# Feed-forward gate and up tiles as seven block products of half the tokens, with sums of weights on GpSimd, in four phases

## What is computed

```python
def swiglu(h, wg, wu, wd):
    return (jax.nn.silu(h @ wg) * (h @ wu)) @ wd
...
for layer in range(DEPTH):
    h = rmsnorm(x, ffn_norm_g[layer, 0])
    x = x + 0.5 * swiglu(h, ffn_w_gate[layer, 0], ffn_w_up[layer, 0], ffn_w_down[layer, 0])
    h = rmsnorm(x, mix_norm_g[layer])
    ...
    h = rmsnorm(x, ffn_norm_g[layer, 1])
    x = x + 0.5 * swiglu(h, ffn_w_gate[layer, 1], ffn_w_up[layer, 1], ffn_w_down[layer, 1])
return rmsnorm(x, final_norm_g)
```

## Time and profile before

| | |
|---|---|
| time, median of 3 runs (lowest to highest) | 2102.38 us (2102.25 to 2102.57) |
| span of the profiled execution, first to last instruction | 2100.5 us |
| PE busy | 2081.9 us, 99% |
| DVE busy | 1205.3 us, 57% |
| ACT busy | 732.8 us, 35% |
| POOL busy | 107.2 us, 5% |
| granted TensorE clock, mean | 1.000 |
| moved by DMA | 195.17 MB, 93 GB/s in the mean |

### The profile page before, as it was taken

How to read it: one execution, slowest core, us unless ns; L and a number is a source line. 1 busy time by engine, 2 the same in 40 slices (tenths; PEclk the granted TensorE clock), 3 DMA queues, 4 the chain that set the end, 5 groups by cost and what they waited for, 6 DMA issues and landing times.

```text
span 2100.5 us, 30045 instructions
## 1 busy us (share of the span) xinstructions
PE 2081.9 (99%) x11183; PEld 1693.5 (81%) x11183; DVE 1205.3 (57%) x1925; ACT 732.8 (35%) x1029; POOL 107.2 (5%) x143
## 2 busy tenths in 40 slices
PE   8999999999999999999999999999999999999998
PEld 6888888788888888888888888888866688888887
DVE  6435445595777896444346544435679855444345
ACT  4212223453445442222124222222467742222223
POOL 0000000001000000000010000000026500000000
PEclk9999999999999999999999999999999999999999
DMA  6333433332253324454453333332310123333321
GB/s 174 100 100 91 112 88 93 92 92 72 61 141 96 86 81 120 103 117 104 110 114 103 100 100 90 100 100 76 110 46 1 41 71 100 92 99 91 100 87 64
DMA packets 357990, 195.17 MB, mean 93 GB/s; under 512 B 14891, under 2 KB 349878, under 8 KB 357894
## 3 DMA queue, kind: packets, MB, share of 16 engines
q1 hardware_dynamic: 355270, 184.21, 30.8%
q0 software_dynamic: 2624, 9.67, 2.9%
HBM read 191.07 MB, written 2.79 MB: 92 GB/s over the span
## 4 chain that ended last, share of the span: by engine, by line
PE 67%; DVE 4%; POOL 2%; issue 1%; ACT 0%; DVEq 0%; ACTq 0%; POOLq 0%
PE ps L1659 18%; PE ps L1657 18%; PE ps L1658 18%; PE ps L2276 1%; PE ps L2247 1%; POOL index_scores L490 1%; PE ps L2226 1%; PE ps L1989 1%; PE ps L1676 1%; PE ps L1991 1%; PE ps L1990 1%; PE ps L1677 1%; PE ps L1678 1%; POOL sq L487 1%; DVE w_lo L904 1%
## 5 line engine op out<-in xcount | busy, mean ns | idle before, releaser
L509 ACT ACTIVATE w_hi<-w_raw 128x1024 fp32r<-128x1024 f32 x351 | 371.7, 1060 | 1011.9 <-PE ps L1659 954.6
L1657 PE MATMUL ps<-h_hi,w_hi 128*128 128x512 f32 x1552 | 605.4, 390 | 0.0
L1658 PE MATMUL ps<-h_lo,w_hi 128*128 128x512 f32 x1552 | 603.8, 389 | 0.0
L1659 PE MATMUL ps<-h_hi,w_lo 128*128 128x512 f32 x1552 | 603.8, 389 | 0.0
L904 DVE TENSOR_TENSOR w_lo<-w_raw,w_hi 128x1024 fp32r<-128x1024 f32 x351 | 429.7, 1225 | 281.4 <-ACT w_hi L509 281.1
L1657 PEld LDWEIGHTS ps<-h_hi,w_hi 128*128 128x128 f32 x1552 | 291.4, 188 | 61.8 <-issue 1.7
L1659 PEld LDWEIGHTS ps<-h_hi,w_lo 128*128 128x128 f32 x1552 | 291.4, 188 | 60.6
L1658 PEld LDWEIGHTS ps<-h_lo,w_hi 128*128 128x128 f32 x1552 | 291.4, 188 | 60.0
L1657 PE MATMUL ps<-act_hi,w_hi 128*128 128x512 f32 x692 | 269.3, 389 | 0.0
L1659 PE MATMUL ps<-act_hi,w_lo 128*128 128x512 f32 x692 | 269.2, 389 | 0.0
L1658 PE MATMUL ps<-act_lo,w_hi 128*128 128x512 f32 x692 | 269.2, 389 | 0.0
(11 more groups left out here) (354 smaller groups left out, 2207.1 us busy)
## 6 DMA issues: line engine op xcount, KB each, us to landing
w_raw<-in_ffn_w_gate SPq DMA_DIRECT2D x88, 512.0 KB, 3.8
w_raw<-in_ffn_w_up SPq DMA_DIRECT2D x88, 512.0 KB, 3.8
w_raw<-in_ffn_w_down SPq DMA_DIRECT2D x64, 512.0 KB, 4.1
w_raw<-in_hy_w_in SPq DMA_DIRECT2D x44, 512.0 KB, 3.8
w_raw<-in_ffn_w_down SPq DMA_DIRECT2D x32, 384.0 KB, 3.5
w_raw<-in_hy_w_out SPq DMA_DIRECT2D x16, 512.0 KB, 3.8
acum_rows<-acum_scratch POOLq DMA_DIRECT2D x4, 1024.0 KB, 10.7
bias_rows<-line_scratch POOLq DMA_DIRECT2D x8, 512.0 KB, 6.8
```

Of the source, the lines that this page charges most:

```text
L509: act.activation(w_hi[:, s, :], w_raw[:, s, :], ACT.Copy).then_inc(hi_ready, 1)
L1657: pe.matmul(ps[:, bank, :], wh, rh[:, k, :], start=k == 0, stop=False)
L1658: pe.matmul(ps[:, bank, :], wh, rl[:, k, :], start=False, stop=False)
L1659: mm = pe.matmul(ps[:, bank, :], wl, rh[:, k, :], start=False, stop=k == nk - 1)
```

## The change

For tiles 2 to 21 of each stage (`PLAIN = 2` tiles stay as before) the gate and the up tile are computed together. The reduction of 1024 is cut in two halves, the tokens in two halves of 256, and gate and up are the two columns of a 2 x 2 block matrix: four blocks by four blocks, which take eight block products, are computed by seven, with sums and differences of the factors (Strassen's scheme).

- **PE** (`seven`): seven products of 4 blocks by 3 matmuls, each matmul 256 columns, in place of two units of 24 matmuls of 512 columns. Bank `BB + j` collects four of the products one upon another, and ACT takes a copy of it after the first, the second and the third (`keep`), bank `BC + j` is copied once; the third, fifth, sixth and seventh product wait for such a copy.
- **POOL**: four subtractions of 128 x 512 for each tile (`weight_sums`) make three mixed weight blocks in `mix_raw` and one in place in `w_raw`; four of 128 x 4 x 256 for each stage (`h_sums`) do so for the activations; and it multiplies each tile's `silu_gate` by `rms_rows` (`weight_gate`).
- **ACT**: `t_high` copies the mixed weights (128 x 1536) to `mix_hi`, four `keep` copies of 128 x 256, `act_hi` in place of DVE; at a stage's start eight scaled copies to `s_raw` and four to `s_hi`.
- **DVE**: `t_low` (128 x 1536), and in place of lines 1034 and 1037 five operations of 128 x 256; at a stage's start four of `s_low`.
- **Phases**: `((0, 6), (6, 6), (12, 6), (18, 4))`, so 8 more down units in each stage, each shorter, and the last phase has 4 blocks for each down unit. Down units start with the last block held back for the first two or three units.
- The loops are written out. `bias_rows` is loaded only after the last product of `ffn2`, since its place is now used by the sums. Several semaphores are merged.

```diff
-PHASES = ((0, 8), (8, 8), (16, 6))
+HC = UC // 2
+PHASES = ((0, 6), (6, 6), (12, 6), (18, 4))
+PLAIN = 2
+BB, BA, BC = 0, 2, 6
...
+            def weight_sums(st, f):
+
+                k = MIXED[st] + f - PLAIN
...
+                pool.wait_ge(raw_landed[u % SLOTS], LAND[u])
+                pool.wait_ge(raw_landed[(u + 1) % SLOTS], LAND[u + 1])
+                if k >= 2:
+                    pool.wait_ge(t_lo_ready, k - 1)
+                pool.tensor_tensor(t[:, 0:HC], up[:, 0:HC], gate[:, 0:HC], ALU.subtract).then_inc(t_made, 1)
+                pool.tensor_tensor(up[:, 0:HC], up[:, HC:UC], up[:, 0:HC], ALU.subtract).then_inc(t_made, 1)
+                pool.wait_ge(t_made, 4 * k + 1)
+                pool.tensor_tensor(t[:, HC:2 * HC], up[:, HC:UC], t[:, 0:HC], ALU.subtract).then_inc(t_made, 1)
+                pool.wait_ge(t_made, 4 * k + 3)
+                pool.tensor_tensor(t[:, 2 * HC:3 * HC], gate[:, HC:UC], t[:, HC:2 * HC], ALU.subtract).then_inc(t_made, 1)
...
+            def weight_gate(st, f):
...
+                pool.wait_ge(silu_done, F + 2)
+                pool.tensor_tensor(silu_gate[:, f % 2, :], silu_gate[:, f % 2, :], rms_rows[:, :], ALU.mult).then_inc(gate_weighted, 1)
...
+                    for f in range(first, end):
+                        if f > first:
+                            weight_gate(st, f - 1)
+                        if f + 2 < end:
+                            weight_sums(st, f + 2)
...
+            def t_high(k):
+                act.wait_ge(t_made, 4 * (k + 1))
+                if k >= 2:
+                    act.wait_ge(prod_done, 5 * (k - 1))
+                act.activation(mix_hi[:, k % 2, :], mix_raw[k % 2], ACT.Copy).then_inc(t_hi_ready, 1)
...
+                    for f in range(max(f0, PLAIN), f0 + nf):
+                        u = n + 2 * (f - f0)
+                        if f > max(f0, PLAIN):
+                            silu(f - 1)
+                        keep(f, 0)
+                        produce_hi(u + 3)
+                        if f < last:
+                            t_high(MIXED[st] + f + 1 - PLAIN)
+                        keep(f, 1)
+                        keep(f, 2)
+                        if f > max(f0, PLAIN):
+                            act_high(f - 1, f0)
+                        keep(f, 3)
+                        produce_hi(u + 4)
...
+                    for f in range(first, last + 1):
+                        u = n + 2 * (f - f0)
+                        if f > first:
+                            gate_high(f - 1)
+                        produce_lo(u + 2)
+                        gate_low(f, u)
+                        if f > first:
+                            product(f - 1)
+                        produce_lo(u + 3)
+                        if f < last:
+                            t_low(MIXED[st] + f + 1 - PLAIN)
+                        if f > first:
+                            act_low(f - 1, f0)
+                        up_sums(f, u)
...
+                def product(dst, w_at, c0, r_at, k0, half, start):
+                    for k in range(4):
+                        wh, wl = (w[:, c0 + k * P:c0 + (k + 1) * P] for w in w_at)
+                        rh, rl = (r[:, k0 + k, HALF[half]] for r in r_at)
+                        pe.matmul(dst, wh, rh, start=start and k == 0, stop=False, skip_group_check=True)
+                        pe.matmul(dst, wh, rl, start=False, stop=False, skip_group_check=True)
+                        mm = pe.matmul(dst, wl, rh, start=False, stop=k == 3, skip_group_check=True)
+                    return mm
...
+                    product(b, gate, 0, h, 0, 0, True).then_inc(prod_done, 1)
...
+                    product(a, gate, HC, h, 4, 0, True).then_inc(unit_used, 1)
+                    pe.wait_ge(t_lo_ready, k + 1)
+                    pe.wait_ge(kept, 4 * k + 1)
+                    if f == PLAIN:
+                        pe.wait_ge(s_lo_ready, 4 * q + 3)
+                    product(b, mixed, HC, sums, 0, 0, False).then_inc(prod_done, 1)
...
+                    product(c, mixed, 0, sums, 4, 1, True).then_inc(prod_done, 1)
+                    pe.wait_ge(lo_ready, u + 2)
+                    pe.wait_ge(kept, 4 * k + 2)
+                    product(b, up, 0, sums, 0, 1, False).then_inc(prod_done, 1)
+                    pe.wait_ge(kept, 4 * k + 3)
...
+                    product(c, up, HC, sums, 4, 0, False).then_inc(unit_used, 1)
+                    pe.wait_ge(kept, 4 * k + 4)
+                    product(b, mixed, 2 * HC, h, 4, 1, False).then_inc(prod_done, 1)
```

More of the change, by code:

```diff
@@ L321, in columns @@
             def columns(n, w, c0, tiles, kt=KT):
-                with sp.Fori(0, tiles // 4) as i:
+                for i in range(tiles // 4):
                     for j in range(4):
-                        load(n + j, i, [(slot(n + j, kt), w[:, :, bass.ds(i * (4 * P) + (c0 + j * P), P)])])
+                        load(n + j, i, [(slot(n + j, kt), w[:, :, c0 + (4 * i + j) * P:c0 + (4 * i + j + 1) * P])])
                 return n + tiles
@@ L565, in ffn @@
                     n += 2 * nf
+                    silu(last)
+                    produce_hi(n + 3)
+                    act_high(last, f0)
                     if st == STAGES[0] and ph == 1:
                         line_out()
-                    if ph < 2:
-                        with act.Fori(0, 2) as i:
-                            for j in range(4):
-                                produce_hi(n + j + SLOTS, i)
+                    if ph < len(PHASES) - 1:
+                        for m in range(1, KT):
+                            produce_hi(n + m + 3)
+                            if m == 6:
+                                t_high(MIXED[st] + f0 + nf - PLAIN)
@@ new lines, in ffn @@
+                for ph, (f0, nf) in enumerate(PHASES):
+                    if ph == 0:
+                        produce_lo(n + 4)
+                        scaled(0)
+                        product(0)
+                        act_low(0, 0)
+                        produce_lo(n + 5)
+                        t_low(MIXED[st])
+                        s_low(0)
+                        s_low(1)
+                        scaled(1)
+                        product(1)
+                        act_low(1, 0)
+                        s_low(2)
+                        s_low(3)
+                    first, last = max(f0, PLAIN), f0 + nf - 1
+                    for f in range(first, last + 1):
[12 more added lines that the diff above has]
+                        up_sums(f, u)
+                    n += 2 * nf
+                    gate_high(last)
+                    produce_lo(n + 2)
+                    product(last)
+                    act_low(last, f0)
+                    if ph < len(PHASES) - 1:
+                        for m in range(KT):
+                            if m:
+                                produce_lo(n + m + 2)
+                            add_x(xc, n, m // 4, m % 4, 0.5)
+                        t_low(MIXED[st] + f0 + nf - PLAIN)
@@ new lines, in ffn @@
+                    together = 2 if nf > 4 else 3
+                    for m in range(together):
+                        down(m, range(0, nf - 1), nf, f0)
+                    for m in range(together):
+                        down(m, range(nf - 1, nf), nf, f0)
+                    for m in range(together, KT if ph < len(PHASES) - 1 or nxt != "final" else KT - 2):
+                        if st == STAGES[0] and ph == 1 and m == 2:
+                            pe.wait_ge(l_ev, 2)
+                            pe.wait_ge(gains_ready, 3)
+                        down(m, range(nf), nf, f0)
```

459 lines of the change are left out of this document (290 added, 169 removed).

## The result

| | before | after |
|---|---|---|
| time, median | 2102.48 us (2102.25 to 2104.24) | 2223.44 us (2223.12 to 2224.63) |
| ratio, 95% interval | | 1.0574 [1.0561, 1.0587] |
| span, mean granted clock of TensorE | 2100.5 us, 1.000 | 2222.8 us, 0.975 |

The account below looks back on a forecast made before the run. PE alone, busy 99%, was taken to set the time. The sum -64 + 45 + 46 + 1.5 + 1 + 1 = +31 made the span 2131 and the median 2133, shifted by 2 to 2135 us; range 2080 to 2185.

Parts of the forecast that it names:

- Gain on PE: Gate and up tiles take 10.08 us in place of 10.88; 20 tiles in 4 stages give -64 us.
- The bound of 10 us for instruction fetch: Written-out loops cost nothing visible; some 10 us should instruction fetch not follow 6720 short matmuls.
- Steady tiles: DVE and POOL take turns reading SBUF; POOL needs 11.5 to 11.8 us a tile, PE waits at product 5: +45 us.
- third rival: DVE and POOL alternate whole instructions, pacing a tile at 12.9 us: 2225 us; chance 0.08 for anything above 2185.
- The start of a stage: At product 3 of a stage's first mixed tile PE waits 11.4 us for `s_lo`, four times: +46 us.
- The wait for `s_lo`: PE at product 3 of each stage's first mixed tile waits 11.4 us for the low parts of activation sums.
- `bias_rows`, +1 (0 to 10): Eight 512 KB loads in one burst from the end of `ffn2`, used some 50 us later, cost 0 to 10, taken as 1.
- Boundaries: DVE falls behind in a stage's last phase; 0 to 3 us, taken as 0.5 for each of three boundaries.
- Second rival: POOL slips into DVE's PSUM work, copies stay in time, only starts lose: 2051, or 2070 to 2090; chance 0.25.

Follow-up runs that it names:

- Experiment 1: Changed kernel, with GpSimd starting a stage's sums only after VectorE has finished the norm's reciprocal root: 2220.23 us (1.0561 of the kernel before).
- 11: Changed kernel with four plain tiles a stage, sums of `h` spread over three tiles, all sums on VectorE, `bias_rows` loaded by SyncE: 2081.65 us (0.9897).
- 12: Changed kernel with four plain tiles, spread sums of `h`, `bias_rows` by SyncE, sums on GpSimd beginning after the root: 2133.50 us (1.0144).
- experiment 3: Changed kernel, with GpSimd's feed-forward sums and products replaced by memsets that only write, same semaphores: 2099.72 us (0.9992 of the kernel before).
- Experiment 9: Changed kernel, with `bias_rows` loads issued by SyncE, two behind each of the four `w_uq` loads: 2197.22 us (1.0446 of the kernel before).
- experiment 8: Kernel before, with only its phases changed to 6, 6, 6 and 4 tiles, no products of halves or sums: 2107.20 us (1.0020).
- 10: Changed kernel with all sums on VectorE, `bias_rows` by SyncE, and two reorderings, at stage starts and in a phase's first mixed tile: 2130.35 us (1.0132).

## Why the prediction was wrong in size and right in sign

The direction, the mechanism and the place of most waits held; three terms were too small and one was missing, and the time is 38 us beyond the range's upper end. The largest parts of the miss are the bias stall (28 us more than forecast), the starts (24) and the steady tiles (8); the lower clock and short waits, for which the sum had next to nothing, are about 30, and PE gained 3 less.

- **Gain on PE, -64:** right; the matmuls' time without waits fell by about 61. The bound of 10 us for instruction fetch had no row behind it, and the matmuls of 256 columns kept their 0.120.
- **Steady tiles, +45:** near, 52.7. The rule read from the earlier trace rows, one after another with some 0.13 us of overlap, gave 11.5 to 11.8 us a tile, and 12.0 came: POOL's 2.2 us means and `w_lo` above 1300 as said. The place was wrong: PE waits at product 3, not 5. The copy of product 1 goes into `silu_gate`, behind the previous tile's SiLU on ACT, and that waits for `gate_high`, which stands on DVE behind the stretched `mix_lo` and `act_lo`. The third rival's 12.9 did not come in the steady tiles, though its total of 2225 did, by other ways.
- **The start of a stage, +46:** the step that failed. It followed one chain, to `s_lo`, and took the time until "the last `x` update and ACT's squares" as given. POOL's sums are released by the same event as the root's chain on DVE, eleven instructions of 0.16 us, each of which can wait for a whole instruction of POOL. The chain took 14.4 us (819.4 to 833.8) in place of 2.1, and the waits at the starts were 70.0 in place of 46. The wait for `s_lo` that I did forecast, 11.4 us four times, came to 13.0 in all, PE having already stood for the root or for `silu_gate`. I had counted exclusive time by the length of DVE's instructions, and not by their number. Experiment 1 shows that the root was only where the shortage came to light; 11 and 12 that it is a shortage of room before the first mixed tile. Why `ffn0` has its 17.0 was not taken apart; 7.0 of them are left in experiment 3.
- **`bias_rows`, +1 (0 to 10):** the second failed step, 28.8. I asked when `bias_rows` is used, some 50 us later, and not what its 4 MB displace: weights that PE wants within some 10 us. Experiment 9 shows it with 26 us.
- **Boundaries, +1.5:** 3.8 by experiment 8.
- **Lower clock and short waits:** not in my sum. PE stopped at 1571.4; its granted clock is 0.80 in the window of 10 us from 1570 and 0.50, its lower level (1.2 GHz), in the next, and it was still 0.50 when PE worked again, from 1590.7 to 1595. After the waits for `rs` PE started at that level too (0.50 from 834 to 838). That is some 19 us of matmuls that took longer, and short waits are some 13 more.
- **Second rival, the covers hold (0.25):** excluded for this placement; that experiment 11 lands in its 2070 to 2090 is chance, since that kernel has no sums on GpSimd to be covered.

The change's idea was sound and its placement was not. The scheme gives up to 0.8 us a tile; sums on GpSimd take 1.27 us each of an input that VectorE needs, where on VectorE itself they take 0.61 from start to start. The Trainium skill (GPSIMD Engine Reference, "Engine selection") names VectorE for elementwise work on a tile, GpSimd being about two times slower with two inputs; the rows agree, 1.27 and 0.69.

## What to carry to other kernels

An engine that shows 5% busy is not free if it shares a read interface with a busy one: count the exclusive time of both together, and the number of short instructions in any chain that runs beside it. Moving work from GpSimd to the busier VectorE made this kernel 52 us faster at nearly the same schedule (12 and 11). Ask of a moved transfer what it stands ahead of, not only when its data are used; and expect a removed wait to come back at the next instruction where an engine has no room, as at the starts of the stages here (1 and 10), until some of its work is taken out or moved to where it has time.

## What the runs showed of the hardware

- A DVE instruction of 4 columns, 0.16 us by itself, took up to 2.27 us beside GpSimd's sums of 2.33: the wait was for the other side's whole instruction, whatever one's own size. It hit an instruction with one input too (1.07 us).
- GpSimd's memsets of 1.28 us each beside VectorE left the mean of `w_lo` unchanged (1222 ns), so it is reading that is shared.
- A two-input subtraction of 512 columns, undisturbed, takes 1.27 us on GpSimd and 0.69 (0.61 from start to start) on VectorE.
- Matmuls of 256 columns start 0.120 us apart and those of 512 columns 0.227, at a granted clock of 1.00.
- While eight loads of 512 KB were queued together, all transfers moved 118 to 131 GB/s at a DMA share of 1.01 to 1.07, from GpSimd's queue and from SyncE's alike. A load of weights beside them took 29.7 us to land in place of 2.7 to 2.9.
